# The first modulation in strips of columns turned by VectorE, and two tiles of the second group brought forward into the first stage

## Chip, core and metric

One core of one Trainium2 chip runs the whole program in one launch. The metric is the device time in microseconds (us). The kernel before took 2163.56 us, the median of 3 runs (2163.24 to 2165.64).

## What is computed

Two layers of one mixer block run over 640 tokens: 512 latent tokens (modulated by a vector c) and 128 context tokens (modulated by c_ctx). The width is D = 2048. The part of the reference that the change touches, for each layer:

```
mod  = silu(cond) @ w_mod[l] + b_mod[l]          # 2048 x 6144, for two vectors: c and c_ctx
shift, scale, gate = split(mod, 3)
xn   = rmsnorm(x, norm_w) * (1 + scale) + shift
proj = xn @ w_in[l]                              # 2048 -> 5664 columns
... attention (8 heads), convolution, gated linear attention (GLA) on parts of proj ...
x    = x + gate * (concat(A, B, C) @ w_out[l])
```

## The kernel before, in words

Everything is float32. A product of full width is made of three products in the fast format fp32r: each operand is split in a high part (rounded) and a low part (the rest), and high*high + high*low + low*high is summed in PSUM. "Cast" below is ScalarE's copy that makes the high part of a weight chunk (L1249), "low" is VectorE's subtraction (L1748).

The work of each layer is: front projection, attention with more projection tiles between its steps (L822), GLA with the first half of the output projection as filling (`fill`, L1050), second half of the output projection (`half_tile`, L843). Each engine has its own program, written out by hand, in fixed order; semaphores join them. SyncE (SP) issues nearly all loads, in order, and a wait in its queue holds all loads behind it.

**Front projection.** 8 groups of 4 tiles (512 columns of `w_in` each). A group walks k, the 2048 rows, in 8 chunks of 2 x 128 rows. So there are 64 chunks, numbered 0 to 63; chunk n belongs to group n // 8. A chunk is one load of 512 KB into a ring of 4 slots (`ring`, L369), one cast, one low, and 5 pieces on TensorE (`front_piece`, L771): one for each of the 4 tiles over the 512 latent tokens, one for the 128 context tokens. A piece is 2 rows of k times 3 products, 6 matmuls of 512 columns. Chunk n can be cast when chunk n - 4, the one before it in its slot, is done on TensorE (L1246). A group's sums stand in PSUM `psP` (4 tiles) and `psT` (context). ScalarE takes them out (`take_group`, L1260) and stores them; it does so in its program after cast 8g + 10, and the first piece of the next group's tile m waits for tile m to be taken (L779).

**First modulation (layer 0, shift and scale).** 32 MB of `w_mod` come through four buffers `wmod` of 1 MB, one for each quarter q of k. They make 8 blocks t of 512 columns; t = 2j and 2j + 1 give scale and shift of the 4 rows of x in block j. `mod_quarter(t, q)` (L695) makes 4 float32 matmuls of 512 columns with the two conditioning vectors as weights; each of the 4 has its own strip of 32 PSUM partitions, so a quarter's k are spread over the strips, and the strips must be summed later. ScalarE copies the result to SBUF (`mod_row`, L1204), TensorE sums the strips and turns them with 4 small matmuls against `fold` (`mod_turn`, L705), ScalarE takes that (`mod_take`, L1211), VectorE adds the bias (`mod_sum`, L1755). Two PSUM places are used in turn. Then ScalarE applies scale and shift to x (L1337) and VectorE splits it (L1784, L1786). TensorE's program (L914 to L929) puts pieces of group 0 between the quarters of t = 2 to 7; the pieces of block j run beside the loads of block j + 1.

**Other modulation.** Gate of layer 0 and shift and scale of layer 1 are summed by VectorE in chunks 8 to 63: 16 units of 4 quarters, a quarter being 8 operations (`mod_quarter` of VectorE, L1704). `quarters_at` (L112) says after which chunk's low they run: 8 quarters in 7 chunks. VectorE may start a unit when TensorE has added up the strips of the unit two before it (L1710; `mod_strips`, L849, at the chunks `STRIPS_AT`). Layer 1 uses the same table for its gate. After chunk 63 VectorE forms x again from its parts (L1885), TensorE reads it in `gate_ranks` (L745), and all engines meet in a fence (L396) before attention.

Of the kernel before, what the change touches and what calls it, by code (L numbers as in the profile page):

```python
# [24 lines left out]
P = 128  # L25
# [3 lines left out]
DEPTH = 2  # L29
# [65 lines left out]
PIECES_AFTER, PIECES_LAST = [0, 2, 0, 2, 0, 2, 0, 1], 3  # L95
assert sum(PIECES_AFTER) + PIECES_LAST == BLOCK_C * PIECES and len(PIECES_AFTER) == 8
# [90 lines left out]
NAMES = """gla_lr_in x_part0 x_part1 rows_in x_in consts_in rows_turned vecs_ready head_ready embed_turned x_taken  # L187
# [7 lines left out]
chunk_in0 chunk_in1 chunk_in2 chunk_in3 chunk_cast chunk_split chunk_done latent_done latent_taken  # L195
# [15 lines left out]
def backbone(nc, io):  # L211
    with ExitStack() as ctx:
# [22 lines left out]
        fold = sb("fold", [P, P // 4])  # L235
# [99 lines left out]
        mod_rows = [sq_sum[:, 0:MOD_N], r_b[:, 0:MOD_N]]  # L335
# [33 lines left out]
        def ring(pair, n):  # L369

            at = n % RING
            return pair[at // 2][:, at % 2 * KT // 2:(at % 2 + 1) * KT // 2, :].rearrange("p a b -> p (a b)")\
                .rearrange("p (k n) -> p k n", n=GROUP_N)
        rs_ps = [psT[:, 0:512], psO[:, 512 + 2 * P:512 + 3 * P]]
        mod_ps, mod_back = [psT[:, 512:512 + MOD_N], psO[:, 0:MOD_N]], psO[:, 512:512 + 2 * BLOCK_K]
# [29 lines left out]
        def _(sp):  # L405
# [18 lines left out]
            def front_chunk(l, n):  # L424

                at = n + l * FRONT_CHUNKS
                first, k = FRONT[n // CHUNKS][0], n % CHUNKS * CHUNK_K
                if n < RING:
                    sp.wait_ge(s[f"split{n // 2}"], l * per_layer + SEED)
                else:  # L430
                    sp.wait_ge(s["chunk_split"], at - RING + 1)
                sp.dma_start(ring(raw, n), io["w_in"][l].rearrange("(k p) n -> p k n", p=P)
                             [:, k:k + CHUNK_K, first * P:first * P + GROUP_N]).then_inc(s[f"chunk_in{n % RING}"], 16)

            for t in range(MOD_CHUNKS):
                mod_block(t)
                front_chunk(0, t)

# [13 lines left out]
            for l in range(DEPTH):  # L452
# [51 lines left out]
                sp.wait_ge(s["chunk_split"], (l + 1) * FRONT_CHUNKS - 2)  # L504
                conv_weights(0, 0)
                value_in(0)
                sp.wait_ge(s["chunk_split"], (l + 1) * FRONT_CHUNKS)
# [177 lines left out]
        def _(pe):  # L685
            def spread(out, lhsT, rhs, start=True, stop=True):

                pe.matmul(out[:, 0:512], lhsT, rhs[:, 0:512], start=start, stop=stop)
                return pe.matmul(out[:, 512:TOK], lhsT, rhs[:, 512:TOK], start=start, stop=stop)

# [4 lines left out]
            def mod_quarter(t, q):  # L695

                if q == 0 and t >= 2:
                    pe.wait_ge(s["mod_row"], t - 1)
# [6 lines left out]
            def mod_turn(t):  # L705

                pe.wait_ge(s["mod_row"], t + 1)
                pe.wait_ge(s["mod_taken"], t + SEED)
                for j in range(BLOCK_K):
                    mm = pe.matmul(mod_back[:, 2 * j:2 * j + 2], mod_rows[t % 2][:, j * P:(j + 1) * P], fold[:, 0:2],  # L710
                                   start=True, stop=True)
                mm.then_inc(s["mod_turned"], 1)
# [5 lines left out]
            pe.wait_ge(s["ones_set"], 4)  # L718
            pe.wait_ge(s["x_in"], 16 * TT)
            pe.wait_ge(s["vecs_ready"], DEPTH)  # L720
# [11 lines left out]
            for q in range(4):  # L732
                mod_quarter(1, q)
                if q == 0:
                    pe.wait_ge(s["x_squared"], 2 * TT + 2)
                    mod_turn(0)
            mod_turn(1)
# [33 lines left out]
            def front_piece(l, n, m):  # L771

                g, c = l * len(FRONT) + n // CHUNKS, n % CHUNKS
                whole, rest = ring(high, n), ring(low, n)
                if m == 0:
                    pe.wait_ge(s["chunk_split"], n + l * FRONT_CHUNKS + 1)
# [23 lines left out]

            def block_piece(n):

                front_piece(0, n // PIECES, n % PIECES)
# [45 lines left out]
            def mod_strips(l, u):  # L849

                pe.wait_ge(s["mod_acc"], u + l * UNITS + 1 + SEED)
                if u == 0:
                    pe.wait_ge(s["mod_taken"], l + MOD_CHUNKS + SEED)
                    pe.wait_ge(s["ones_set"], 4 + 3 * (l + 1))
# [9 lines left out]
            def units_turn(l):  # L864

                pe.wait_ge(s["mod_row"], l + MOD_CHUNKS + 1)
# [29 lines left out]
            for l in range(DEPTH):  # L896
# [13 lines left out]
                else:  # L910
# [3 lines left out]
                    for t in range(2, MOD_CHUNKS):  # L914
                        for q in range(4):
                            mod_quarter(t, q)
                            if t % 2 == 1 and q == 0:
                                mod_turn(t - 1)
# [3 lines left out]
                        if t % 2 == 1:  # L922
                            mod_turn(t)
# [3 lines left out]
                    while piece < CHUNKS * PIECES:  # L927
# [153 lines left out]
                for pr in range(PAIRS):  # L1081
# [109 lines left out]
        def _(act):  # L1191
# [12 lines left out]
            def mod_row(t):  # L1204

                act.wait_ge(s["wmod_used3"], t + 1 + SEED)
                if t >= 2:
                    act.wait_ge(s["mod_turned"], t - 1)
                act.activation(mod_rows[t % 2], mod_ps[t % 2], ACT.Copy).then_inc(s["mod_row"], 1)

            def mod_take(t):  # L1211

                act.wait_ge(s["mod_turned"], t + 1)
                act.activation(mod_raw[:, 0, mod_at(t):mod_at(t) + BLOCK_K, :].rearrange("p a b -> p (a b)"), mod_back,
                               ACT.Copy).then_inc(s["mod_taken"], 1)

# [10 lines left out]
            for l in range(DEPTH):  # L1227
                act.wait_ge(s["rows_turned"], l + 2)
                act.activation(vecs[:, l, :], psP[l][:, 0:ROWS], ACT.Copy).then_inc(s["vecs_ready"], 1)
# [11 lines left out]
            def cast_ring(l, n):  # L1241

                at = n + l * FRONT_CHUNKS
                act.wait_ge(s[f"chunk_in{n % RING}"], 16 * (at // RING + 1 + l * SLOT_FILLS[n % RING]))
                if n >= RING:
                    act.wait_ge(s["chunk_done"], at - RING + 1)  # L1246
                elif l > 0:
                    act.wait_ge(s[f"tile_done{n // 2}"], l * per_layer - 1 + n % 2 + SEED)
                act.activation(ring(high, n), ring(raw, n), ACT.Copy).then_inc(s["chunk_cast"], 1)  # L1249

            for l in range(DEPTH):
# [7 lines left out]

                def take_group(g):  # L1260
# [3 lines left out]
                    for m in range(GROUP_T):  # L1264
# [1023 lines left out]
```

## Time and profile before

| what | value |
|---|---|
| median of 3 runs | 2163.56 us |
| profiled execution, its own time | 2162.03 us |
| its span | 2160.1 us |
| TensorE (PE) busy | 2118.3 us, 98% |
| VectorE (DVE) busy | 1403.7 us, 65% |
| ScalarE (ACT) busy | 649.2 us, 30% |
| GpSimd (POOL) busy | 190.6 us, 9% |
| mean DMA rate | 168 GB/s |
| first 54 us / next 54 us of the span | 355 / 387 GB/s |

The profiled execution lasted 1.93 us longer than its span. A busy TensorE isn't TensorE at its peak: the matmuls overlap, and the time of a stretch is read from start to start. A line that is that of a helper stands for many places; tiles and times tell them apart.

### The profile page before, as it was taken

What the parts mean: (1) busy time and instruction counts of PE and PEld (TensorE: products, weight loads), DVE (VectorE), ACT (ScalarE), POOL (GpSimd) and SP (SyncE); (2) the same over time, 40 slices, a digit from 0 to 9 for tenths busy, and PEclk for the clock granted to TensorE, in tenths of its full rate; (3) what the DMA queues carried; (4) which work ended last, traced back from release to release, by engine and by line L of the source; (5) the groups of instructions that cost most, each with busy time, mean ns of one, the idle gap of its engine ahead of it and who ended that gap; (6) DMA issues with size and microseconds to landing.
All of it is one profiled execution on the core that took longest, in us unless ns stands there. A gap on an engine that the chain in (4) does not pass through costs nothing.

```text
span 2160.1 us, 33866 instructions
## 1 busy us (share of the span) xinstructions
PE 2118.3 (98%) x13255; PEld 1886.6 (87%) x13255; DVE 1403.7 (65%) x2739; ACT 649.2 (30%) x1104; POOL 190.6 (9%) x125
## 2 busy tenths in 40 slices
PE   5999999999999999999999999999999999999998
PEld 3578887887999999999998888888899999999998
DVE  5469878999565666765357555455666566676654
ACT  4332221321333334443034122132133333343302
POOL 0000000000000000423321000000000000042331
PEclk9999999999999999999999999999999999999999
DMA  9999687664433324564445646544343233366444
GB/s 355 387 309 307 197 287 244 210 217 153 121 105 89 100 87 130 186 212 129 127 125 173 190 139 193 151 131 132 113 129 104 75 97 105 99 210 195 140 123 151
DMA packets 355216, 363.25 MB, mean 168 GB/s; under 512 B 17606, under 2 KB 262044, under 8 KB 354460
## 3 DMA queue, kind: packets, MB, share of 16 engines
q1 hardware_dynamic: 326416, 318.57, 47.4%
q10 hardware_dynamic: 28684, 43.09, 5.5%
q8 instruction: 78, 1.28, 0.2%
q14 instruction: 38, 0.31, 0.0%
HBM read 302.89 MB, written 58.72 MB: 167 GB/s over the span
## 4 chain that ended last, share of the span: by engine, by line
PE 89%; DVE 4%; DMA 3%; issue 2%; ACT 1%; ACTq 0%; SPq 0%; DVEq 0%
PE psP L787 32%; PE psP L822 20%; PE psP L843 9%; PE psT L797 8%; PE psO L1050 5%; PE psO L1023 3%; PE psP L978 2%; PE psT L1050 2%; DMA wmod<-in_w_mod_dram 2%; PE psT L989 2%; DVE old L2021 1%; PE psT L701 1%; PE psP L725 1%; PE psO L859 1%; DVE second_low L1690 0%
## 5 line engine op out<-in xcount | busy, mean ns | idle before, releaser
L1730 DVE SCALAR_TENSOR_TENSOR macc<-mraw,cond,macc 128x384 f32<-128x384 f32 (+1 forms) x960 | 389.1, 476 | 0.0
L787 PE MATMUL psP<-x_high,high 128*128 128x512 f32 x896 | 356.2, 398 | 0.6 <-DVE x_low L1786 0.6
L787 PE MATMUL psP<-x_high,low 128*128 128x512 f32 x896 | 349.8, 390 | 0.0
L787 PE MATMUL psP<-x_low,high 128*128 128x512 f32 x896 | 349.8, 390 | 0.0
L1249 ACT ACTIVATE high<-raw 128x1024 fp32r<-128x1024 f32 x128 | 135.5, 1059 | 550.3 <-PE psT L797 512.8
L822 PE MATMUL psP<-x_high,high 128*128 128x320 f32 x1024 | 242.6, 318 | 0.0
L822 PE MATMUL psP<-x_high,low 128*128 128x320 f32 x1024 | 233.4, 309 | 0.0
L822 PE MATMUL psP<-x_low,high 128*128 128x320 f32 x1024 | 233.1, 309 | 0.0
L787 PEld LDWEIGHTS psP<-x_high,high 128*128 128x128 f32 x896 | 168.6, 188 | 49.4 <-issue 10.5
L1748 DVE TENSOR_TENSOR low<-raw,high 128x1024 fp32r<-128x1024 f32 x128 | 163.1, 1274 | 73.5 <-ACT high L1249 73.5
L787 PEld LDWEIGHTS psP<-x_high,low 128*128 128x128 f32 x896 | 168.6, 188 | 35.9
L787 PEld LDWEIGHTS psP<-x_low,high 128*128 128x128 f32 x896 | 168.8, 188 | 33.9 <-issue 0.5
L822 PEld LDWEIGHTS psP<-x_high,low 128*128 128x128 f32 x1024 | 171.1, 188 | 0.0
L822 PEld LDWEIGHTS psP<-x_low,high 128*128 128x128 f32 x1024 | 171.0, 188 | 0.0
L822 PEld LDWEIGHTS psP<-x_high,high 128*128 128x128 f32 x1024 | 167.5, 188 | 0.6 <-issue 0.5
L2191 POOL MEMSET cu<- 128x643 f32 x2 | 1.3, 635 | 1588.0 <-DVEq L396 1588.0
L1050 PE MATMUL psO<-x_high,high 128*128 128x320 f32 x704 | 134.8, 313 | 2.1 <-DVE old L2021 2.1
L1720 DVE TENSOR_SCALAR macc<-mraw,cond 128x384 f32<-128x384 f32 (+1 forms) x64 | 19.7, 349 | 158.0 <-PE psO L859 129.7
L843 PE MATMUL psP<-second_high,high 128*128 128x320 f32 x512 | 116.9, 310 | 1.8 <-DVE low L1683 1.8
L843 PE MATMUL psP<-second_low,high 128*128 128x320 f32 x512 | 116.8, 309 | 0.0
L843 PE MATMUL psP<-second_high,low 128*128 128x320 f32 x512 | 116.6, 309 | 0.0
L1050 PEld LDWEIGHTS psO<-x_high,high 128*128 128x128 f32 x704 | 109.4, 188 | 6.1 <-DVE old L2021 3.9
(319 smaller groups left out, 3615.6 us busy)
## 6 DMA issues: line engine op xcount, KB each, us to landing
raw<-in_w_in_dram SPq DMA_DIRECT2D x128, 512.0 KB, 4.9
wmod<-in_w_mod_dram SPq DMA_DIRECT2D x32, 1024.0 KB, 9.9
mraw<-in_w_mod_dram SPq DMA_DIRECT2D x64, 512.0 KB, 4.3
mraw<-in_w_mod_dram SPq DMA_DIRECT2D x32, 1024.0 KB, 7.6
raw<-in_w_in_dram SPq DMA_DIRECT2D x32, 1024.0 KB, 6.2
raw<-in_w_out_dram SPq DMA_DIRECT2D x64, 512.0 KB, 4.5
old<-x_scratch SPq DMA_DIRECT2D x64, 320.0 KB, 3.2
xf<-proj_scratch SPq DMA_DIRECT2D x48, 320.0 KB, 3.6
```

The source lines that it names most:

```text
L701: mm = pe.matmul(mod_ps[t % 2][32 * k:32 * k + 2, :], cond[:, q * KT // 4 + k, :], wmod[q][:, k, :], start=(q == 0), stop=(q == 3), skip_g ...
L787: mm = pe.matmul(latent_ps[m], own, moved, start=(k == 0 and w is whole and x is x_high), stop=(k == KT - 1 and w is rest))
L797: mm = pe.matmul(prompt_ps, x[:, k, DEC:TOK], w[:, kk, :], start=(k == 0 and w is whole and x is x_high), stop=(k == KT - 1 and w is rest))
L822: mm = pe.matmul(psP[0][:, AT + half * HALF:AT + (half + 1) * HALF], w[slot][:, k, :], x[:, k, half * HALF:(half + 1) * HALF], start=(k == ...
L843: mm = pe.matmul(out[:, AT + half * HALF:AT + (half + 1) * HALF], w[slot][:, at + k, :], x[:, k, half * HALF:(half + 1) * HALF], start=(k ...
L978: mm = pe.matmul(score_ps[:, part], q[:, i * P:(i + 1) * P], x[:, part], start=(q is q_high and x is k_high), stop=(q is q_low))
L989: mm = pe.transpose(psT[:, j * P:(j + 1) * P], probs[i % 2][:, j * P:(j + 1) * P], ident[:])
L1023: pe.matmul(psO[:, 0:DEC], v[:, j, :], x[:, j, :], start=(j == 0 and v is vals_high and x is probs_high), stop=(j == KEYS // P - 1 and v i ...
L1050: mm = pe.matmul(out[:, AT + half * HALF:AT + (half + 1) * HALF], w[slot][:, at + k, :], x[:, k, half * HALF:(half + 1) * HALF], start=(k ...
L1249: act.activation(ring(high, n), ring(raw, n), ACT.Copy).then_inc(s["chunk_cast"], 1)
L1730: m = dve.scalar_tensor_tensor(acc[:, v, 0:width], mraw[hf][:, k, 0:width], c, acc[:, v, 0:width], ALU.mult, ALU.add)
L1748: dve.tensor_tensor(ring(low, n), ring(raw, n), ring(high, n).bitcast(F32), ALU.subtract)\
```

## The change

The constants:

```diff
-PIECES_AFTER, PIECES_LAST = [0, 2, 0, 2, 0, 2, 0, 1], 3
+EXTRA_T, EXTRA_PIECES = 2, 4
+PIECES_AFTER, PIECES_LAST = [0, 2, 1, 2, 1, 2, 1, 2], 3
+EXTRA_SLOT = RING - 1
```

**First modulation.** Every k now makes 4 matmuls of 128 columns, one for each strip b; strip b holds the columns 32b to 32b + 31 of each of the 4 rows, and all k are added up in PSUM. One VectorE transpose of 32 x 32 blocks gives the result turned. `mod_row`, `mod_turn`, `mod_take` and `fold` are gone. There is one PSUM place, not two, so quarter (t, 0) waits for the turn of t - 1.

```diff
+                if q == 0 and t > 0:
+                    pe.wait_ge(s["mod_turned"], t)
                 pe.wait_ge(s[f"wmod_in{q}"], t * 16 + 16)
                 for k in range(KT // 4):
-                    mm = pe.matmul(mod_ps[t % 2][32 * k:32 * k + 2, :], cond[:, q * KT // 4 + k, :], wmod[q][:, k, :],
-                                   start=(q == 0), stop=(q == 3), skip_group_check=True)
+                    at = q * KT // 4 + k
+                    parts = wmod[q][:, k, :].rearrange("p (j b c) -> p b j c", b=P // FLIP, c=FLIP)
+                    for b in range(P // FLIP):
+                        mm = pe.matmul(mod_ps[FLIP * b:FLIP * b + 2, :], cond[:, at, :], parts[:, b],
+                                       start=(at == 0), stop=(at == KT - 1), skip_group_check=True)
...
+                    def flip(t):
+                        dve.wait_ge(s["wmod_used3"], t + 1 + SEED)
+                        dve.transpose(mod_turn[t % 2], mod_ps).then_inc(s["mod_turned"], 1)
...
                     scale_block(0)
-                    chunk_low(0)
                     for j in range(BLOCKS):
+                        flip(2 * j)
+                        chunk_low(BLOCK_C * j)
+                        flip(2 * j + 1)
+                        dve.wait_ge(s["mod_turned"], 2 * j + 2)
...
+                        dve.wait_ge(s["chunk_cast"], extra_turn(j) + 1)
+                        dve.tensor_tensor(extra_slot(low), extra_slot(raw), extra_slot(high).bitcast(F32), ALU.subtract)\
+                            .then_inc(s["chunk_split"], 1)
```

**Two tiles of group 1.** Its tiles 0 and 1 walk all of k in the first stage, 4 pieces a block, between the chunks 2j and 2j + 1, into `psO`. Their weights (4 loads of 512 KB) use slot 3 of the ring; group 0 has 3 slots. So a chunk of group 0 frees slot n % 3, and chunk 9 (slot 1) now waits for chunk 7. In group 1 the chunks have 3 pieces in place of 5; they are loaded and cast in full.

```diff
+def slot_user(l, n):
+    if n < RING:
+        return n - EXTRA_SLOT if l == 0 and n >= EXTRA_SLOT else None
+    if l == 0 and n < CHUNKS:
+        return n - EXTRA_SLOT
+    if l == 0 and n < CHUNKS + RING:
+        return [m for m in range(CHUNKS) if chunk_slot(0, m) == n % RING][-1] if n % RING < EXTRA_SLOT else "extra"
+    return n - RING
...
             def cast_ring(l, n):
+                user = slot_user(l, n)
+                if user == "extra":
+                    act.wait_ge(s["extra_done"], BLOCKS)
+                elif user is not None:
+                    act.wait_ge(s["chunk_done"], user + l * FRONT_CHUNKS + 1)
...
                 for n in range(FRONT_CHUNKS):
                     if l > 0 or n >= CHUNKS:
-                        for m in range(PIECES):
+                        for m in range(EXTRA_T if l == 0 and n // CHUNKS == 1 else 0, PIECES):
                             front_piece(l, n, m)
...
+                    if l == 0 and n == CHUNKS + RING:
+                        for e in range(EXTRA_T):
+                            take_latent(1, e, extra_ps[e])
```

In the stretch left out above, VectorE adds the bias and splits x as before (`mod_sum`, four `split_x`, chunk 2j + 1's low between them).

**VectorE's quarters**, in both layers: 4 in the 8 chunks of group 1, then 60 in 48 chunks.

```diff
+    def done(j):
+        return j * 4 // CHUNKS if j <= CHUNKS else 4 + (j - CHUNKS) * 4 * (UNITS - 1) // (MOD_SPAN - CHUNKS)
-    return range(j * 4 * UNITS // MOD_SPAN, (j + 1) * 4 * UNITS // MOD_SPAN) if j >= 0 else range(0)
+    return range(done(j), done(j + 1)) if j >= 0 else range(0)
```

**GLA and output projection**, in both layers (the first wait of the second pair stands ahead of the product `qt`, the second ahead of `kt_`):

```diff
-                        fill(f + 7, 0, 1)
+                        fill(f + 7, 0, 2)
                         turn_back(gp)
-                        fill(f + 7, 1, HALF_K)
+                        fill(f + 7, 2, HALF_K)
...
-                    dve.wait_ge(s["g_factors"], gp * 2 + 2)
+                    dve.wait_ge(s["g_factors"], gp * 2 + 1)
...
+                    dve.wait_ge(s["g_factors"], gp * 2 + 2)
...
-                    low_half(f + 5)
+                        if i == TT - 3:
+                            low_half(f + 5)
...
+                second_weights(0, 1)
                 for j in range(2):
                     sp.wait_ge(s[f"x_part{j}"], 16 * (l + 1) * OUT_PAIRS + SEED)
-                for j in range(2):
-                    old_x(j, 0)
-                with sp.Fori(1, OUT_PAIRS) as i:
-                    for j in range(2):
-                        second_weights(j, i)
-                        sp.wait_ge(s[f"taken{j}"], i + occ + SECOND + SEED)
-                        old_x(j, i)
+                    old_x(j, 0)
+                with sp.Fori(1, OUT_PAIRS - 1) as i:
+                    second_weights(1, i)
+                    sp.wait_ge(s["taken0"], i + occ + SECOND + SEED)
+                    old_x(0, i)
+                    second_weights(0, i + 1)
+                    sp.wait_ge(s["taken1"], i + occ + SECOND + SEED)
+                    old_x(1, i)
...
```

## Rows read from the trace of the kernel before

**Rows 1.** A stretch: length, busy us (instructions) by engine, TensorE's clock, DMA share, GB/s
```profile
49.00:56.00 7.00, 6.43 (x22) 3.50 (x25) 6.90 (x11) 2.40 (x4) 0.00 (x0) 0.57 1.05 387
```
**Rows 2.** Timeline of TensorE, one block: start, length, engine, line, operation [idle before]
```profile
86.33 1.05 PE L710 MATMUL psO<-fold,sq_sum 128*128 128x2 f32 x8
87.32 1.04 PE L701 MATMUL psO<-wmod,cond 128*2 128x512 f32 x8
...
92.61 1.04 PE L701 MATMUL psO<-wmod,cond 128*2 128x512 f32 x8 [0.34 <-DMA wmod<-in_w_mod_dram]
...
95.08 0.95 PE L710 MATMUL psO<-fold,r_b 128*128 128x2 f32 x8
95.88 0.49 PE L787 MATMUL psP<-x_high,high 128*128 128x512 f32 x1
...
110.71 1.05 PE L710 MATMUL psO<-fold,sq_sum 128*128 128x2 f32 x8
```
**Rows 3.** The chain that ended last, in order of time: start, us, what
```profile
131.40 5.44 PE psP L787 x24
138.20 5.44 PE psP L787 x24
...
414.70 5.44 PE psP L787 x24
```
**Rows 4.** Timeline of TensorE after the front projection
```profile
536.37 1.29 PE L745 MATMUL psO<-xf,lr_w 128*32 128x160 f32 x32 [0.26 <-DVE x_last L1885]
```
**Rows 5.** Timeline of the start, all engines
```profile
39.66 3.03 DVE L1793 TENSOR_TENSOR x_hat<-xf,rstd 128x640 f32<-128x640 f32 x4
39.73 4.53 SPq L421 DMA_DIRECT2D wmod<-in_w_mod_dram  x4
...
49.56 1.88 PE L701 MATMUL psT<-wmod,cond 128*2 128x512 f32 x8 [1.59 <-DMA wmod<-in_w_mod_dram]
51.38 0.80 PE L787 MATMUL psP<-x_high,high 128*128 128x512 f32 x1
```
**Rows 6.** Timeline of ScalarE where group 0 ends
```profile
135.06 1.06 ACT L1249 ACTIVATE high<-raw 128x1024 fp32r<-128x1024 f32 x1 [0.26 <-DMA raw<-in_w_in_dram]
136.03 0.58 ACT L1268 ACTIVATE stage<-psP 128x512 f32<-128x512 f32 x1
...
138.23 0.60 ACT L1268 ACTIVATE rstd<-psP 128x512 f32<-128x512 f32 x1 [0.51 <-ACT stage L1268]
```
**Rows 7.** Timeline of VectorE in the front projection
```profile
138.51 1.22 DVE L1748 TENSOR_TENSOR low<-raw,high 128x1024 fp32r<-128x1024 f32 x1
139.65 4.32 DVE L1730 SCALAR_TENSOR_TENSOR macc<-mraw,cond,macc 128x384 f32<-128x384 f32 x8
...
411.88 1.47 DVE L1837 SCALAR_TENSOR_TENSOR xf<-xf 128x1280 f32<-128x1280 f32 x1
...
414.79 8.55 DVE L1730 SCALAR_TENSOR_TENSOR macc<-mraw,cond,macc 128x384 f32<-128x384 f32 x16
...
428.83 0.75 DVE L1720 TENSOR_SCALAR macc<-mraw,cond 128x384 f32<-128x384 f32 x2 [2.95 <-PE psO L859]
...
511.73 1.23 DVE L1748 TENSOR_TENSOR low<-raw,high 128x1024 fp32r<-128x1024 f32 x1 [0.47 <-ACT high L1249]
...
521.34 1.22 DVE L1659 CAST high<-raw 128x2048 fp32r<-128x2048 f32 x1
```
**Rows 8.** Timeline where attention begins
```profile
550.74 0.28 DVE L1897 TENSOR_TENSOR vals_low<-cv,vals_high 128x128 fp32r<-128x128 f32 x1
...
553.55 0.45 PE L978 MATMUL psP<-k_high,q_high 128*128 128x320 f32 x2
```
**Rows 9.** Waits of TensorE over the span: us in total, times, longest
```profile
PE psO L1050 <- DVE old L2021: 2.1, 8, 0.3
PE psP L843 <- DVE low L1683: 1.8, 2, 1.0
PE psT L1070 <- DVE kt_ L2071: 1.5, 2, 1.1
```

More of the change, by code:

```diff
@@ L334, in backbone @@
                 ytok = sb("ytok", [P, TT, D], F32, last)
-        mod_rows = [sq_sum[:, 0:MOD_N], r_b[:, 0:MOD_N]]
+        mod_turn = [sq_sum[:, i * P:(i + 1) * P] for i in range(2)]
         unit_rows = sq_sum[:, 0:MOD_STEP * P // 2]
@@ L799, in front_piece, with extra_piece @@
                 mm.then_inc(s["chunk_done"], 1)
-            def block_piece(n):
-                front_piece(0, n // PIECES, n % PIECES)
+            def extra_piece(j, i):
+                e, pair = i % EXTRA_T, i // EXTRA_T
+                whole, rest = extra_slot(high), extra_slot(low)
+                if i == 0:
+                    pe.wait_ge(s["x_split"], (j + 1) * BLOCK_K + SEED)
+                    pe.wait_ge(s["chunk_split"], extra_turn(j) + 1)
+                cols = slice(e * P, (e + 1) * P)
+                for kk in range(2 * pair, 2 * pair + 2):
+                    k = j * BLOCK_K + kk
+                    for w, x in ((whole, x_high), (whole, x_low), (rest, x_high)):
+                        mm = pe.matmul(extra_ps[e], w[:, kk, cols], x[:, k, 0:DEC],
+                                       start=(k == 0 and w is whole and x is x_high), stop=(k == KT - 1 and w is rest))
+                if i == EXTRA_PIECES - 1:
+                    mm.then_inc(s["extra_done"], 1)
+            def block_piece(n):
+                j, i = n // BLOCK_PIECES, n % BLOCK_PIECES
+                if i < PIECES:
+                    front_piece(0, BLOCK_C * j, i)
+                elif i < PIECES + EXTRA_PIECES:
+                    extra_piece(j, i - PIECES)
+                else:
+                    front_piece(0, BLOCK_C * j + 1, i - PIECES - EXTRA_PIECES)
             def turn_prompt(g):
@@ L926, in _ @@
                                 piece += 1
-                    while piece < CHUNKS * PIECES:
+                    while piece < BLOCKS * BLOCK_PIECES:
                         block_piece(piece)
@@ L1258, in cast_chunk, with take_latent @@
                     cast_ring(l, n)
+                def take_latent(g, m, src):
+                    first, gate = FRONT[g]
+                    n = l * len(FRONT) + g
+                    tile = n * GROUP_T + m
+                    act.wait_ge(s[f"stored{m % 2}"], (n * GROUP_T // 2 + l * HEADS) * 16 + SEED)
+                    if tile // EXTRA_T == GROUP_T // EXTRA_T:
+                        act.wait_ge(s["extra_done"], BLOCKS)
+                    else:
+                        act.wait_ge(s["latent_done"], tile + 1 - (EXTRA_T if tile > GROUP_T else 0))
+                    act.activation(leaving[m], src, ACT.Silu if gate else ACT.Copy).then_inc(s["latent_taken"], 1)
+                    act.wait_ge(s["latent_taken"], tile + 1)
+                    dst = v_dram[m] if g == BY_TOKEN else proj_dram[first + m][:, 0:DEC]
+                    act.dma_start(dst, leaving[m]).then_inc(s[f"stored{m % 2}"], 16)
                 def take_group(g):
@@ L1263, in take_group @@
                     n = l * len(FRONT) + g
-                    for m in range(GROUP_T):
-                        tile = n * GROUP_T + m
-                        act.wait_ge(s[f"stored{m % 2}"], (n * GROUP_T // 2 + l * HEADS) * 16 + SEED)
-                        act.wait_ge(s["latent_done"], tile + 1)
-                        act.activation(leaving[m], latent_ps[m], ACT.Silu if gate else ACT.Copy)\
-                            .then_inc(s["latent_taken"], 1)
-                        act.wait_ge(s["latent_taken"], tile + 1)
-                        dst = v_dram[m] if g == BY_TOKEN else proj_dram[first + m][:, 0:DEC]
-                        act.dma_start(dst, leaving[m]).then_inc(s[f"stored{m % 2}"], 16)
+                    for m in range(EXTRA_T if l == 0 and g == 1 else 0, GROUP_T):
+                        take_latent(g, m, latent_ps[m])
                     act.wait_ge(s["chunk_done"], (n + 1) * CHUNKS)
@@ L1597, in _ @@
             dve.memset(ones[:], 1.0).then_inc(s["ones_set"], 1)
-            for part in mod_ps:
-                dve.memset(part, 0.0).then_inc(s["ones_set"], 1)
+            dve.memset(mod_ps, 0.0).then_inc(s["ones_set"], 1)
             dve.wait_ge(s["consts_in"], 16 * 5)
-            dve.tensor_reduce(fold[:], ident[:].rearrange("p (a b) -> p b a", a=4), AX.X, ALU.add).then_inc(s["ones_set"], 1)
             def set_pick():
```

148 lines of the change are left out of this document (76 added, 72 removed).

## The prediction

> **What bounds the kernel now.** The page first: TensorE is busy 98% of the span, at full clock in all 40 slices but for one place, so a change gains only what it takes off TensorE's own queue or off its waits. I then read the chain of waits: it is TensorE nearly throughout, at an even pace. A chunk's 30 matmuls of 512 columns take 138.20 - 131.40 = 6.80 us [rows 3], so one piece (6 matmuls) costs 1.36. The first stage is the exception. There the DMA engines are full (share 1.05, 387 GB/s [rows 1]), and TensorE is nearly full too: from one turn to the same turn a block later is 110.71 - 86.33 = 24.38 us [rows 2], with about 0.4 us of wait for data in it (0.34 in the row, a little more by the starts). Two limits are balanced there; removing TensorE work alone would only turn it into waiting for the 9 MB of a block. Last the waits of TensorE: outside the first 50 us they are short, the three that the late edits address being 2.1, 1.8 and 1.5 us in all [rows 9].
>
> **Turns removed, tiles moved in.** The moved tiles are no saving by themselves: 16 pieces x 1.36 = 21.8 us go from group 1 to group 0. They matter because they fill the room that the turns leave. In a block the two `mod_turn` cost 87.32 - 86.33 = 0.99 and 95.88 - 95.08 = 0.80 us [rows 2]. A new block costs TensorE 24.38 - 1.79 - 0.4 + 4 x 1.36 = 27.6, and there are two more places where it goes from pieces to a quarter and back, for which I take 0.3 each, an estimate (the matmul after such a change shows 0.49 us against a pitch of 0.227 [rows 2, 3]): 28.2. The loads of a block grow from 9 to 9.5 MB, 24.38 x 9.5 / 9 = 25.7 us, so they stay below 28.2, and the waits for data go. Gain per block 24.38 + 5.44 - 28.2 = 1.6, for three blocks **-4.8 us**. Bounds: -6.6 if a change of kind costs nothing, -2 if it costs 0.8.
>
> **The quarters in strips.** A quarter has 16 matmuls of 128 columns (32 records) in place of 4 of 512 (8 records): the same columns. The nearest row is `gate_ranks`, also four strips of short float32 matmuls: 32 records of 160 columns in 1.29 us [rows 4], by 128/160 1.03 us, as long as the 1.04 of an old quarter [rows 2]. I take **0**. Upper bound: 1.29 in full, 0.25 x 22 quarters = +5.5; lower bound 0, since no column is saved.
> The Trainium skill ("TensorE: Matmul & The Clock Gate", section "Wait — 56ns, not 53.3ns?") speaks against the change here: start to start never drops below about 25 ns, and with hardware decode off the sequencer spends about 62 ns for each matmul. By the 62 ns a quarter would be 32 x 62 = 1.98 us, and the sum would be some 22 us worse. The row, 1.29 us / 32 = 40 ns for longer matmuls, disagrees with 62 and leaves the 25 open.
>
> **VectorE's turn in place of ScalarE's copies.** A transpose of 128 columns is not in the trace; ScalarE's and TensorE's part that it replaces was off the path but for the turns. Between 0.2 and 1 us each; in blocks 1 to 3 it stands behind five pieces or two (6.8 or 2.7 us), which hide it. VectorE's block (2 turns, sums, 4 splits, 3 lows, 3.03 us of scaling) is about 15 us of 28, so it is not late. Exception: t = 1. One PSUM place means that quarter (1, 0) waits for the turn of t = 0, which stands behind the scaling of block 0, 39.66 + 3.03 = 42.7 [rows 5]. TensorE ran it at once before. So the buffers come free near 43.9 in place of 39.73 [rows 5]. The DMA engines still have chunk 1 and now 0.5 MB for the moved tiles in queue, so they idle only about 1.5 us; quarter (2, 1) comes at about 51.0 in place of 49.56 [rows 5], and the first piece moves from 51.38 likewise: **+1.4** (0 to +4; the upper end if the clock, 0.57 in this stretch [rows 1], falls during the longer lull and quarter t = 1 runs at half pace).
>
> **The hand-over from group 0 to group 1.** Chunk 9 now uses the slot of chunk 7, so its cast waits for TensorE's last piece of group 0. In ScalarE's program cast 9, cast 10, then the four takes follow one another. TensorE's next piece is tile 2 of chunk 8, which waits for three takes. Cast to next operation is 136.03 - 135.06 = 0.97, take to take (138.23 - 136.03) / 2 = 1.10 [rows 6]. So: 0.2 + 2 x 0.97 + 2 x 1.10 + 0.60 = 4.9, with the signal 5.0 us in which TensorE has nothing to do. Before, the takes lay in the time of the last pieces: chunk 8 began at 138.20 [rows 3] with the first take done at 136.6. **+5.0**. Upper bound +8.4, if the clock falls after this lull for as long as at 48 to 55 us (0.57 over 7 us is 3.4 us lost if busy); I put **+1.0** for it. Lower bound +3.9 (a shorter queue of takes).
>
> **Quarters of VectorE.** A low costs 139.65 - 138.51 = 1.14, a quarter 8.47 / 2 = 4.24, the first of a unit 3.84 [rows 7]. Group 1's chunks now last 3 x 1.36 = 4.1 us, and half a quarter each fits (3.3). After it, 4 chunks hold 5 quarters: 4 x 1.14 + 5 x 4.24 - 0.5 = 25.3, against 4 x about 7.1 = 28.4 us of TensorE; with the key normalisation some 4 us more in places. So VectorE isn't the bound but lives with little room, and it ends later. Unit 11 now begins at chunk 48, after the strips of chunk 46, about 415.4 (chunk 47 starts at 414.70 [rows 3]). Against the kernel before at 414.79 it has still to do one quarter (3.84), one low (1.14), the 414.79 - 411.88 = 2.91 us of chunk 49, and in chunks 49 to 63 one quarter more (19 for 18, and less 0.4 for an earlier unit start: 3.8); it saves the three waits of 2.95, 4.18 and 0.47 = 7.6 us [rows 7] (the first and last of the three). End of the quarters: 521.34 + 0.6 + 3.84 + 1.14 + 2.91 + 3.8 - 7.6 = 526.0 to 526.5, some 5 us later. The forming of x (16 operations) and the fence before attention follow it. TensorE waited 0.26 us for it already [rows 4]. Where attention begins, VectorE's last preparation ended at 551.02 and TensorE's scores began at 553.55 [rows 8]: 2.4 us of slack. **+2.6** (0 to +6). Layer 1's quarters are a third as wide; nothing there.
>
> **Late edits.** The weights of tile 1 no longer stand in SP's queue behind the stores: the 1.8 us [rows 9] go, what is late next is the add before it, hidden by a half tile. The factor product starts one exponential (1.25 us) earlier: the 1.5 us for `kt_` go. `low_half` in an idle place of VectorE: of the 2.1 us some 1.2 go. The turn back stands one k (0.9 us) later; its chain has about 1 us of slack: 0. Together **-4.5** (-5.4 to -1.5).
>
> **Sum.** -4.8 + 0 + 1.4 + 5.0 + 1.0 + 2.6 - 4.5 = +0.7 us. On the profiled execution's own time 2162.03 (2160.1 span and 1.9 around it) that is 2162.7; the runs' median is 1.5 higher, so 2163.56 + 0.7, **2164.3 us**: no change that can be told. A measurement of this kernel can tell about 0.2%, 4.3 us.
>
> **Rivals.**
> (a) Faster: the hand-over costs little, because TensorE would otherwise have waited there or the takes run sooner, and VectorE's lag is absorbed. Then -4.8 + 1.4 - 4.5 = -7.9, **2155.7**. For it: the two main costs are read from program order, not from a row. Against: each link of the hand-over is a wait that stands in the diff. 0.33.
> (b) Slower, one mechanism: VectorE becomes the bound of groups 2 to 7. From 48 chunks x 7.1 = 341 us it needs 48 x 1.14 + 60 x 4.24 - 6 + 13 (keys) = 316, plus its waits for strips and for `mraw`. If these waits exceed 25 us (40 were spent before), each further us is TensorE's. With 8 more, 2164.3 + 8 = **2172**. It decides from a low that ends after its chunk could start; I reckon the smallest margin at 2 us. 0.19.
> (c) The short matmuls are bound by their issue: +5.5, **2170**. 0.06. By the skill's 62 ns it would be 2186, which I put at 0.01 within this.
> (d) The first stage stays bound by loads (3 slots, queue of SP), so the new pieces displace nothing: +5, **2169**. 0.05.
> The forecast has 0.37, with its own range 2160 to 2168.
>
> **How the numbers follow.** Faster (below 2159.3): nearly all of (a) and a little of the forecast, 0.35. Slower (above 2167.9): most of (b), (c), (d) and the forecast's edge, 0.28. Same: 0.37. The range 2154 to 2173 takes (a) and (b) in and leaves out 0.2.
>
> **What would show it.** No L710 rows, and blocks of about 28 us with no wait for `wmod` after 55 us; quarters of 0.9 to 1.1 us. An idle stretch of about 5 us of TensorE before the first piece of chunk 8, ended by ScalarE's take L1268 (its line may shift), with the clock after it. VectorE's last quarter some 5 us late against TensorE's chunk 63, and a wait of TensorE for x in `gate_ranks`. No TensorE wait of over 0.5 us in GLA. The forecast is wrong if that stretch is absent, or if chunks 16 to 63 show waits for a low.

## The result, and the profile after

The changed kernel takes **2167.04 us** (median of 20 runs, 2165.74 to 2170.15), the kernel before 2163.47 (20 runs, 2162.30 to 2165.64). The ratio is 1.0018 (95% interval 1.0012 to 1.0024): slower by 3.9 us, small but clear of the noise. The forecast was 2164.3 in a range of 2154 to 2173. The profiled execution took 2167.36 us, its span 2165.6, 5.5 longer than that of before.

The waits of TensorE over the span, as in [rows 9] (us in total, times, longest):

```profile
...
PE psP L839 <- ACT rstd L1332: 4.9, 1, 4.9
PE psO L755 <- DMA head_rows<-in_final_norm_w_dram: 4.3, 1, 4.3
PE psT L766 <- DVE sq_sum L1871: 4.3, 1, 4.3
PE psT L766 <- DMA wmod<-in_w_mod_dram: 3.8, 2, 2.6
PE psO L1123 <- DVE old L2108: 2.0, 4, 0.7
...
```

Two of them are new: 4.9 us for the third take of group 0 (`rstd` is its buffer), and 4.3 us for the turn of t = 0 (`sq_sum` holds `mod_turn`). The waits for `kt_` and for the low of the second half are gone.

The timeline of TensorE, the start and one block, to be held against [rows 2] and [rows 5]:

```profile
37.82 0.39 PE L787 MATMUL psO<-r_a,ones 128*128 128x128 f32 x2
42.48 5.82 PE L766 MATMUL psT<-wmod,cond 128*2 128x128 f32 x128 [4.27 <-DVE sq_sum L1871]
49.47 1.06 PE L766 MATMUL psT<-wmod,cond 128*2 128x128 f32 x32 [1.17 <-DMA wmod<-in_w_mod_dram]
53.15 1.36 PE L766 MATMUL psT<-wmod,cond 128*2 128x128 f32 x32 [2.62 <-DMA wmod<-in_w_mod_dram]
54.44 0.80 PE L839 MATMUL psP<-x_high,high 128*128 128x512 f32 x1
...
103.62 0.50 PE L839 MATMUL psP<-x_high,high 128*128 128x512 f32 x1
...
110.64 1.93 PE L766 MATMUL psT<-wmod,cond 128*2 128x128 f32 x64
112.50 0.50 PE L839 MATMUL psP<-x_high,high 128*128 128x512 f32 x1
...
132.03 0.50 PE L839 MATMUL psP<-x_high,high 128*128 128x512 f32 x1
```

A block now takes 132.03 - 103.62 = 28.41 us, with no wait for data. Two quarters take 112.50 - 110.64 = 1.86 us with the change to the next piece in it, 29 ns for each of the 64 records on average. Where quarters stand back to back they start 0.87 us apart, and 0.86 us in the kernel before: the strips cost nothing that counts. The records don't come evenly: four start within 0.02 us of each other, one for each strip, and the next four 0.109 us later. The first piece comes at 54.44 in place of 51.38.

Stretches of the start and of the hand-over, columns as in [rows 1]:

```profile
40.00:42.00 2.00, 0.00 (x0) 0.00 (x0) 2.00 (x3) 0.00 (x0) 0.00 (x0) 0.52 1.06 399
42.00:44.00 2.00, 1.52 (x32) 1.06 (x36) 1.53 (x3) 0.35 (x1) 0.00 (x0) 0.50 1.01 354
44.00:46.00 2.00, 2.00 (x44) 1.40 (x40) 0.00 (x0) 0.71 (x1) 0.00 (x0) 0.50 0.36 66
46.00:48.00 2.00, 2.00 (x64) 1.55 (x56) 0.00 (x0) 0.00 (x0) 0.00 (x0) 0.77 0.94 333
...
158.00:163.00 5.00, 0.16 (x1) 0.00 (x0) 3.66 (x7) 3.68 (x5) 0.00 (x0) 1.00 0.25 29
163.00:166.00 3.00, 2.90 (x7) 2.35 (x8) 2.54 (x4) 1.43 (x3) 0.00 (x0) 0.50 0.98 371
```

While TensorE waits for the turn, its clock falls to 0.50; the first two quarters of t = 1 then take 1.7 us each (they start at 42.48 and 44.14, the third at 45.84) in place of 0.87, the buffers come free late, and the loads sink to 66 GB/s. After the 5 us at 158 the clock is 0.50 again.

ScalarE's timeline at the hand-over, to be held against [rows 6]:

```profile
158.26 2.00 ACT L1311 ACTIVATE high<-raw 128x1024 fp32r<-128x1024 f32 x2 [11.16 <-PE psT L849]
160.17 0.58 ACT L1332 ACTIVATE stage<-psP 128x512 f32<-128x512 f32 x1
...
161.26 0.60 ACT L1332 ACTIVATE stage<-psP 128x512 f32<-128x512 f32 x1 [0.52 <-ACT stage L1332]
...
162.36 0.60 ACT L1332 ACTIVATE rstd<-psP 128x512 f32<-128x512 f32 x1 [0.51 <-ACT stage L1332]
```

It shows each link of the forecast: two casts in 1.91 us, started when TensorE ends group 0, then three takes 1.10 apart. TensorE begins again at 163.10, as the third ends.

VectorE: the turn that TensorE waited for, and the end of its quarters (compare [rows 7]):

```profile
39.16 3.03 DVE L1866 TENSOR_TENSOR x_hat<-xf,rstd 128x640 f32<-128x640 f32 x4
42.11 0.31 DVE L1871 STREAM_TRANSPOSE sq_sum<-psT 128x128 f32<-128x128 f32 x1
...
521.87 8.56 DVE L1803 SCALAR_TENSOR_TENSOR macc<-mraw,cond,macc 128x384 f32<-128x384 f32 x16
530.34 1.22 DVE L1732 CAST high<-raw 128x2048 fp32r<-128x2048 f32 x1
```

Where the difference of the two profiled executions arises, by the start of the same matmul on TensorE:

| point | before | after | difference |
|---|---|---|---|
| first piece of group 0 | 51.38 | 54.43 | +3.05 |
| context piece of chunk 63 | 533.89 | 538.75 | +4.86 |
| first filling in GLA, layer 0 | 852.13 | 858.10 | +5.97 |
| layer 0's second half, its 145th matmul | 1016.65 | 1020.81 | +4.16 |
| context piece of chunk 0, layer 1 | 1124.02 | 1130.40 | +6.38 |
| end of layer 1's second half | 2139.82 | 2143.71 | +3.89 |
| end of the span | 2160.1 | 2165.6 | +5.5 |

### The profile page after: what moved, and what is told of

Read it like the earlier page. It is cut to its first block, busy times and chain, and to the rows that moved or that the text cites. A ratio compares the mean times of both kernels' runs of the same rounds, so it can differ in the third digit from the quotient of the medians.

```text
span 2165.6 us, 35256 instructions
## 1 busy us (share of the span) xinstructions
PE 2117.5 (98%) x13959; PEld 1903.3 (88%) x13959; DVE 1412.2 (65%) x2749; ACT 647.7 (30%) x1092; POOL 194.2 (9%) x125
## 4 chain that ended last, share of the span: by engine, by line
PE 88%; DVE 8%; issue 2%; DMA 1%; ACT 1%; ACTq 0%; SPq 0%; DVEq 0%
PE psP L839 27%; PE psP L896 20%; PE psP L917 10%; PE psT L849 7%; PE psO L1123 6%; DVE macc L1803 3%; PE psT L1123 3%; PE psO L1096 3%; PE psP L1051 3%; PE psT L1062 2%; PE psT L766 1%; PE psO L864 1%; DVE low L1821 1%; DVE xf L1972 1%; PE psP L781 0%
## 5 line engine op out<-in xcount | busy, mean ns | idle before, releaser
L839 PE MATMUL psP<-x_high,high 128*128 128x512 f32 x864 | 343.7, 398 | 5.0 <-ACT rstd L1332 4.9
L839 PE MATMUL psP<-x_high,low 128*128 128x512 f32 x864 | 337.5, 391 | 0.0
L839 PE MATMUL psP<-x_low,high 128*128 128x512 f32 x864 | 337.5, 391 | 0.0
L839 PEld LDWEIGHTS psP<-x_high,high 128*128 128x128 f32 x864 | 162.9, 189 | 46.7 <-issue 12.2
L839 PEld LDWEIGHTS psP<-x_high,low 128*128 128x128 f32 x864 | 162.8, 188 | 34.8
L839 PEld LDWEIGHTS psP<-x_low,high 128*128 128x128 f32 x864 | 163.0, 189 | 32.9 <-issue 0.5
L896 PEld LDWEIGHTS psP<-x_high,low 128*128 128x128 f32 x1024 | 171.1, 188 | 0.0
L896 PEld LDWEIGHTS psP<-x_low,high 128*128 128x128 f32 x1024 | 171.0, 188 | 0.0
L896 PEld LDWEIGHTS psP<-x_high,high 128*128 128x128 f32 x1024 | 167.6, 188 | 0.6 <-issue 0.5
```

The source lines that it names most:

```text
L839: mm = pe.matmul(latent_ps[m], own, moved, start=(k == 0 and w is whole and x is x_high), stop=(k == KT - 1 and w is rest))
L896: mm = pe.matmul(psP[0][:, AT + half * HALF:AT + (half + 1) * HALF], w[slot][:, k, :], x[:, k, half * HALF:(half + 1) * HALF], start=(k == ...
```

## The experiments

All ratios are to the kernel before, timed on the same chip; experiments 1 to 4, 5 to 8 and 9 to 11 ran on three different chips, so that times of different groups are compared by their ratios.

**1. The late edits alone**, put into the kernel before (the fourth block of the diff above and nothing else).

> The kernel before with the late edits alone (weights of tile 1 ahead of the stores, the split wait of the factor product, low_half in the loop, the turn back one k later). Theory: they give what the two profiles show between GLA and the end of the second half, 0.6 + 1.2 us in layer 0 and 1.4 + 1.1 us in layer 1, so 4.3 us: 2159.2, ratio 0.998. Rival: the gain in the changed kernel belongs to another phase of the work, and alone they give under 1 us: ratio 0.9995 or more.

2159.35 us, ratio 0.9981 (0.9972 to 0.9990): 4.1 us gained, as the theory has it. No wait for `kt_` or for a low of the second half is left. So the rest of the change costs 0.37%, 8.0 us.

**2. The takes ahead of the cast of chunk 9**, in the changed kernel:

```diff
                 for n in range(RING + (KT - CAST_FROM) // 2, FRONT_CHUNKS + RING):
+                    if l == 0 and n == CHUNKS + 1:
+                        for m in range(GROUP_T):
+                            take_latent(0, m, latent_ps[m])
```

(and `take_group(0)` leaves them out)

> The changed kernel, but the four takes of group 0's latent tiles stand ahead of the cast of chunk 9 in ScalarE's program. Theory: the idle stretch of TensorE at the hand-over (5.1 us) and the half clock after it (1.6 us) are this order of ScalarE alone, both go: 2167.0 - 6.7 = 2160.3. Rival: TensorE then waits for the cast and the low of chunk 9 or 10 or their loads, or VectorE's lag grows by what TensorE gains and comes back at the start of attention: only 2 to 3 us, 2164.5.

2159.43 us, ratio 0.9983 (0.9974 to 0.9992): 7.6 us less than the changed kernel. ScalarE now takes each tile while TensorE works on the next, and casts chunk 9 when group 0 ends:

```profile
153.40 0.60 ACT L1332 ACTIVATE stage<-psP 128x512 f32<-128x512 f32 x1 [5.72 <-PE psP L839]
...
156.12 0.60 ACT L1332 ACTIVATE rstd<-psP 128x512 f32<-128x512 f32 x1 [0.76 <-DMA proj_scratch<-stage]
...
158.84 2.01 ACT L1311 ACTIVATE high<-raw 128x1024 fp32r<-128x1024 f32 x2 [0.76 <-PE psT L849]
```

TensorE has no idle stretch there and no half clock after it. The gain was above the 6.7 of the two; in the profiled executions a stretch at the lower clock where layer 1 begins was shorter as well (3.4 against 6.8 us).

**3. The turn of t = 0 ahead of the scaling of block 0**, in the changed kernel:

```diff
+                    flip(0)
                     scale_block(0)
                     for j in range(BLOCKS):
-                        flip(2 * j)
+                        if j > 0:
+                            flip(2 * j)
```

> The changed kernel, but VectorE turns t = 0 ahead of the scaling of block 0. Theory: TensorE's wait of 4.3 us before quarter (1, 0) shrinks to about 1.2 us, the buffers come free 3 us earlier, the clock keeps its full level there, and the first piece starts at 51.4 in place of 54.4: 2167.0 - 3.0 = 2164.0. Rival: the first piece is bound by the 32 MB that come anyway, the loads of t = 2 are not sooner: under 0.7 us, 2166.5.

2165.38 us, ratio 1.0007 (0.9998 to 1.0016): 2.4 us less by the ratios, whose intervals just touch, near the theory's 3.0. The wait fell to 1.3 us and the clock stayed full while t = 1 ran, but the first piece started at 53.68, not 51.4: TensorE now waits 5.2 us for the first load of t = 2, and the clock falls in that wait instead, for 10.4 us from 47.1 us on.

**4. Both moves together.**

> The changed kernel with both moves (takes ahead of cast 9, turn of t = 0 ahead of the scaling). Theory: the two add up, 2167.0 - 9.7 = 2157.3, ratio to the kernel before 0.9971. Rival: VectorE, whose quarters end later than before, becomes the bound once TensorE is 10 us earlier, and the wait for x before attention takes 3 us or more back: 2160.5.

2157.59 us, ratio 0.9971 (0.9960 to 0.9982), 10.2 us less than the changed kernel by the ratios: they add up. VectorE did not take anything back beyond the wait of 0.5 us for `x_last`.

**5. Strips and turn without the moved tiles**: `EXTRA_PIECES` = 0, group 0 with four slots, the old pieces and the old table of quarters; the late edits stay.

> The first modulation in strips with VectorE's turn, and the late edits, but no moved tiles: group 0 has its 4 slots, the old pieces after each quarter and the old table of VectorE's quarters. It is to be held against the late edits alone (2159.35). Theory: the loads of 9 MB bound the block of 24.4 us, so the 1.8 us of turns per block become waits for wmod: -0.5 a block; the ramp costs some 2 us as before: 2160. Rival: the loads had followed TensorE, not led it, and a block shrinks by the whole 1.8 us: 2156.

2160.46 us, ratio 0.9989 (0.9980 to 0.9998): 1.7 us above experiment 1 by the ratios, with intervals that overlap. The theory had the sum right and its parts not: a block takes, context piece to context piece, 99.33 - 76.27 = 23.1 and then 23.9 us, against 24.35 in experiment 1, but the ramp (the time up to the first piece) is worse: the first piece starts at 55.06 against 52.75. Waits of TensorE up to 130 us, experiment 1, then this one:

```profile
PE psT L707 <- DMA wmod<-in_w_mod_dram: 2.9, 2, 1.6
PE psO L707 <- DMA wmod<-in_w_mod_dram: 1.7, 3, 1.1
PE psO L716 <- ACT r_b L1215: 0.7, 1, 0.7
```

```profile
PE psT L756 <- DMA wmod<-in_w_mod_dram: 6.1, 6, 2.8
PE psT L756 <- DVE sq_sum L1852: 4.3, 1, 4.3
```

The turns had cost 1.8 us a block; about half of it came back as shorter blocks, the rest as waits for `wmod`.

**6. VectorE's old table of quarters** in the changed kernel:

```diff
-    return range(done(j), done(j + 1)) if j >= 0 else range(0)
+    return range(j * 4 * UNITS // MOD_SPAN, (j + 1) * 4 * UNITS // MOD_SPAN) if j >= 0 else range(0)
```

> The changed kernel with the table of VectorE's quarters of before (8 quarters in 7 chunks from chunk 8 on). Theory: group 1's chunks last 4.1 us, 8 lows and 9 quarters need 8 x 1.14 + 9 x 4.24 = 47 us against 33 of TensorE and 10 of lead, so TensorE waits some 4 to 6 us in chunks 11 to 15, and the lag before attention (1.0) goes: 2171, and waits of TensorE for low in group 1. Rival: the lead of VectorE at the hand-over covers it: 2166.

2169.08 us, ratio 1.0027 (1.0017 to 1.0038): 2 us more than the changed kernel, in the right direction and half of what was expected, but the two intervals overlap. The trace shows the mechanism: TensorE waited for a low in chunks 15 and 16, and no longer for `x_last` in layer 0. Part of the cost in the trace is the clock: at the hand-over it was low for 6.9 us (from 161.6 us on) in place of 3.4. Its waits from 158 to 200 us:

```profile
PE psP L839 <- ACT rstd L1332: 4.9, 1, 4.9
PE psP L839 <- DVE low L1821: 1.7, 1, 1.7
```

**7. The first load of the moved tiles behind the loads of t = 2**, on top of both moves:

```diff
                 mod_block(t)
+                if t == 2:
+                    extra_tiles(0)
                 front_chunk(0, t)
-                if t % 2 == 1:
+                if t % 2 == 1 and t > 1:
                     extra_tiles(t // 2)
```

> The kernel with both moves, and the moved tiles' first load put behind the four wmod loads of t = 2 in SP's queue. Theory: the first piece of group 0 waits for the second quarter of t = 2, which stands behind these 0.5 MB; it comes 1.4 us earlier, and so does everything behind: 2157.6 - 1.4 = 2156.2. Rival: x_low of block 0 comes last there (0.6 us was waited for it): 0.3 us, 2157.3.

2157.37 us, ratio 0.9975 (0.9965 to 0.9984): no difference to experiment 4. The first piece did start 1.36 us earlier (51.63 against 52.99). But the clock differs; stretches of experiment 4, then of this one:

```profile
50.00:52.00 2.00, 1.42 (x28) 0.69 (x24) 1.97 (x4) 1.77 (x3) 0.00 (x0) 0.50 1.05 407
52.00:54.00 2.00, 2.00 (x36) 1.45 (x25) 1.97 (x3) 0.00 (x0) 0.00 (x0) 0.89 1.05 398
```

```profile
50.00:52.00 2.00, 2.00 (x33) 1.25 (x26) 1.97 (x4) 0.80 (x2) 0.00 (x0) 0.50 1.06 398
52.00:54.00 2.00, 2.00 (x6) 1.54 (x6) 1.13 (x2) 0.00 (x0) 0.00 (x0) 0.50 1.04 396
54.00:56.00 2.00, 2.00 (x7) 1.60 (x6) 0.00 (x0) 0.00 (x0) 0.00 (x0) 0.60 1.08 399
```

The first pieces came earlier into a stretch at half clock, which lasted 6.9 us here and 3.4 there; the context piece of chunk 15 starts at 187.78 against 187.30. So in this pair of profiles the clock took the 1.4 us back. Over all runs the mean granted clocks of the two kernels (0.9965 here, 0.9961 there) don't show such a loss, so whether this holds for the medians stays open.

**8. VectorE's quarters end two chunks earlier**, on top of experiment 7 (`MOD_SPAN - CHUNKS - 2` in `done`, and at most 64).

> As load_late, and the last 60 quarters of VectorE end two chunks earlier (46 chunks in place of 48). Theory: VectorE's forming of x and its preparation of attention are late by 1.0 us because its last quarters end late; with 4 us or more of lead the waits for x_last (0.5) and for the first scores (0.4) go in layer 0: 1 us below load_late. Rival: the closer quarters make TensorE wait for a low near chunk 32, where the margin was 1.4 us: 1 to 2 us above load_late.

2156.62 us, ratio 0.9973 (0.9962 to 0.9984): not to be told from experiment 7. In the trace layer 0's wait for `x_last` is gone and one for a low of 0.2 us is new; either theory's effect was too small to be timed.

**9 and 10. The stall alone**, in the kernel of experiment 1. `stall_one` has the first edit, `stall_three` both:

```diff
-                    act.wait_ge(s["chunk_done"], at - RING + 1)
+                    act.wait_ge(s["chunk_done"], at - RING + 1 + (2 if at == CHUNKS + 1 else 0))
...
-                        pe.wait_ge(s["latent_taken"], (g - 1) * GROUP_T + m + 1)
+                        pe.wait_ge(s["latent_taken"], (g - 1) * GROUP_T + m + 1 + (2 if n == CHUNKS and m == 0 and l == 0 else 0))
```

> The late edits alone (2159.35), and in group 0's hand-over the cast of chunk 9 waits for chunk 7 as in the changed kernel; TensorE's first piece of chunk 8 waits for one take. Theory, the same links as in the forecast: 0.2 + 2 casts x 0.97 + one take 0.6 = 2.8 us idle, the later takes (1.10 apart) come within the pieces of 1.36; with no or little fall of the clock 2162.2 to 2163.0. Rival: the wait for chunk 7 costs nothing as long as the weights of chunk 8 are split, since casts and takes are short: 2159.5.

> As stall_one, and TensorE's first piece of chunk 8 waits for three takes, as in the changed kernel. Theory: 2.8 + 2 x 1.10 = 5.0 us idle, and with the fall of the clock after it 1.6 or more: 2159.35 + 6.6 = 2166.0, the whole of what the move of the takes gave back in the changed kernel. Rival: the clock falls only because the first stage of the changed kernel already held low stretches; here it holds: 2164.4.

2163.13 us (ratio 0.9997, 0.9988 to 1.0006) and 2166.36 (1.0011, 1.0002 to 1.0020), against 2159.35: 3.8 and 7.0 us by the medians, 3.5 and 6.5 us by the ratios. The wait that TensorE gained in each:

```profile
PE psP L793 <- ACT stage L1274: 2.7, 1, 2.7
```

```profile
PE psP L793 <- ACT rstd L1274: 4.9, 1, 4.9
```

2.7 and 4.9 us of waiting, and in both the clock falls to its lower level for 3.4 us after it. So the stall costs about 7 us in the old surroundings too, and the rival about the clock falls.

**11. Experiment 5 with the turn of t = 0 first.**

> turn_only (strips turned by VectorE, late edits, no moved tiles) with the turn of t = 0 ahead of the scaling. It is to be held against the kernel with both moves (2157.6), which has the moved tiles as well. Theory: the ramp comes 2 us earlier than in turn_only, the blocks stay bound by their loads: 2158.4, so that the moved tiles are worth about 1 us. Rival: the moved tiles bring nothing or cost, since TensorE's room was already used up: 2157.0 or less.

**2156.41 us**, ratio 0.9964 (0.9950 to 0.9977), 5.4 us less than experiment 5 by the ratios, and the lowest median of all (5 runs; experiments 4, 7 and 8 can't be told from it). Against the kernel with both moves, which has the moved tiles too (0.9971), there is no clear difference; the number is the rival's. In the profiled executions the moved tiles do bring the context piece of chunk 15 forward, 187.30 against 189.77; at the end of the span, 2155.8 against 2156.1, little of it is left. Of the 2.5 us experiment 4 loses 0.9 between chunk 63 and GLA, where VectorE is late, and it has two stretches of 3.4 us at the lower clock (from 1107.1 and from 2137.9 us on) that experiment 11 has not. So this one pair of profiles doesn't say that the moved tiles are worth nothing. Against experiment 1 the strips and the turn, well placed, are worth 3.7 us by the ratios, whose intervals overlap a little.

## Why the prediction was right, and where it was not

The time and the reason were near: a gain in the first stage and in the late edits, given back by a stall of ScalarE's order. That the total came so near is in part luck: the forecast lacked two terms (+2.2 and +1.6) and had the ramp too low, while VectorE's term was 1.5 too high. By its steps, in the two profiled executions, whose own times differ by more (5.3 us) than the medians (3.6):

| step | forecast | measured |
|---|---|---|
| first stage | -4.8 | -4.8 |
| quarters in strips | 0 | 0 |
| ramp | +1.4 | +3.05 |
| hand-over, idle | +5.0 | +5.1 |
| clock after it | +1.0 | +1.6 |
| VectorE's lag before attention | +2.6 | +1.1 |
| late edits | -4.5 | -4.2 |
| lower clock at the start of layer 1 | none | +2.2 |
| end of the program | none | +1.6 |
| sum | +0.7 | +5.5 |

The last column adds up to 5.65; the rest is rounding and 0.1 us that layer 1's front projection took less.

- **First stage.** From the first piece to the end of group 0 it was 138.03 - 51.38 = 86.65 us (the first matmul of chunk 8 starts at 138.03; the 138.20 of [rows 3] is where the chain changes over). Now it is 158.00 - 54.43 = 103.57 (its last matmul starts at 157.77, one pitch of 0.23 earlier) with 16 pieces (21.76) more: -4.8. It isn't three equal blocks: -2.1 up to the context piece of chunk 1, then -1.4 and -1.3 for a block, and nothing in the last stretch. The block took 28.41 against the forecast 28.2, so a change between quarters and pieces cost (28.41 - 27.63) / 2 = 0.4 us where the forecast had 0.3 (27.63 is its sum without these changes).
- **Strips.** A quarter with the change to a piece behind it took 0.97 from start to start in the kernel before, now 0.93 to 0.99; back to back it is 0.86 and 0.87. The Trainium skill ("TensorE: Matmul & The Clock Gate", section "Wait — 56ns, not 53.3ns?") tells of about 62 ns for each matmul with hardware decode off and a floor near 25 ns; the 62 ns do not hold here, whether one counts records (0.87 us / 32 = 27 ns) or the program's matmuls (0.87 us / 16 = 55 ns). The mean of 27 ns lies above the floor, but single starts do not: records of different strips start 7 ns apart. By the 62 ns and the forecast's own 22 quarters the loss would have been 0.94 x 22 = 20.7 us, not 22.
- **Ramp.** This step failed in its size. The forecast had the DMA engines idle for 1.5 us; they fell to 66 GB/s at 44 to 46 us and to 305 at 48 to 50. The missing term is the clock: it fell while TensorE waited for the turn, the first two quarters of t = 1 ran at half pace (the upper end of the forecast's range), and quarter (2, 1) came at 53.15, not 51.0. Experiments 3 and 4, whose code is the same up to there, take that wait away and have the first piece at 53.68 and 52.99, so 0.8 to 1.4 of the 3.05 us are shown to come from the place of the turn. What the rest is stays open. Experiment 7 takes 1.36 us by moving the additional load back, but experiment 11, which has no such load, has its first piece at 53.73, no earlier than experiment 4. The start of the turn of t = 0 alone differs by up to 0.9 us between kernels that are the same up to it (42.11 here, 42.97 in experiment 6).
- **Hand-over.** Right in each link: from the start of group 0's last matmul (157.77) to that of the next (163.10) it is 5.33 us, less the pitch of 0.23 that is 5.1 us of idle. Experiments 9 and 10 rebuild it elsewhere and get 2.7 and 4.9. The term for the clock was a little low: 12 matmuls of chunk 8 took 4.35 us in place of 2.72, +1.6 for +1.0. (Its upper bound took 0.57 over 7 us as 3.4 us lost; that is 7 x 0.43 = 3.0.) Experiment 2 takes all of it away.
- **VectorE.** Its quarters end at 530.3, 9.0 us later, and TensorE is 4.9 us later at chunk 63, so its lag grew by 4.1 us; the forecast had 4.7 to 5.2. Another 1.1 us of it is made up before attention: VectorE's last preparation ends at 558.96 against 551.02, 3.1 us late against TensorE. The slack was about what the forecast took: from there to the first scores it was 2.53 us by [rows 8] (the forecast wrote 2.4) and is 559.32 - 558.96 = 0.36 now. So it was the lag that the forecast had too large, not the slack that it had too small, and only 1.1 us came (0.5 of it the wait for `x_last`). It is not the bound of groups 2 to 7: the smallest margin of a low was 1.4 us at chunk 32 (forecast 2), and TensorE waited for none. Rival (b) did not happen. Experiment 6, whose old table brings waits of up to 1.7 us, shows how near VectorE is to being the bound at the end of group 1 and the start of group 2, not in the groups after.
- **Late edits.** 5.97 - 4.16 = 1.8 us in layer 0, 6.26 (where its gate begins) - 3.89 = 2.4 in layer 1; experiment 1 has 4.1 by itself. The split was off: the wait for `old` stayed at 2.0 us, while the second half gained 1.2 and 1.1 us.
- **Not in the forecast.** In the changed kernel's profile the clock is 0.50 from 1116 to 1122 us, at layer 1's start, where it was 1.00 before:

```profile
1114.00:1116.00 2.00, 1.81 (x14) 1.54 (x12) 0.11 (x1) 1.60 (x2) 0.00 (x0) 0.82 0.00 0
1116.00:1118.00 2.00, 2.00 (x9) 2.00 (x10) 0.74 (x5) 0.21 (x1) 0.00 (x0) 0.50 0.00 0
1118.00:1120.00 2.00, 2.00 (x12) 2.00 (x11) 0.00 (x0) 0.00 (x0) 0.00 (x0) 0.50 0.00 0
```

The same work takes longer there (30 transposes, L970, 4.35 us for the 3.51 of before): matmul for matmul, TensorE's delay against the kernel before grows from 4.2 to 7.2 us, and 0.8 of it comes back right behind. The instructions there are the same in both kernels. Over all runs the mean granted clock was 0.9948 in the changed kernel (20 runs) and 0.9966 in the kernel before (29 runs beside experiments 1 to 4); 0.0018 x 2165 / 0.5 = 7.8 us more at the lower level, worth at most 3.9 us. Part of that is the ramp and the hand-over. Why the clock falls at the layer's start in some kernels and executions (in the changed kernel and in experiments 2, 3, 4 and 8; not in the kernel before nor in 1, 5, 6, 7, 9, 10 and 11) stays open.

The end of the program was 1.6 us longer, and the profiles speak against chance. From the start of the last matmul of layer 1's second half to the end of the span it is 20.3 us in the profiles of the kernel before and of experiments 1, 9 and 10, which have the old first modulation, and 21.5 to 22.1 us in the changed kernel and in experiments 2 to 8 and 11, which have the new one. TensorE isn't the cause: in the changed kernel it does this stretch in the same time. The stores of the output are issued no later, but the last of them lands 21.45 us after that start in place of 19.89. Why they take longer stays open.

Rival (a) is ruled out by the row of 4.9 us, (c) by the quarters of 0.87 us, (d) by blocks with no wait for `wmod`.

## What to carry to other kernels

When work is moved from one phase into another, go through each queue at the seam: here a slot's new predecessor made one cast wait, and everything behind it in ScalarE's program, the takes that TensorE needed, came late; moving four instructions was worth 7.6 us, more than any other part of the change (the late edits 4.1, strips and turn 3.7). Before moving work, try the change without it: strips and turn alone, with the first turn ahead of the scaling, could not be told from the version with the moved tiles. A stall is to be priced with the clock after it, 1 to 2 us more here than the stall itself.

## What the runs showed of the hardware that was not expected

- Float32 matmuls of 128 columns and 2 weight columns, laid in four strips, start four at a time, 7 ns apart; the next four start after 109 ns at full clock and after 213 ns at the lower one (t = 1 of the changed kernel). The time follows the clock, so a fixed time for each matmul is not what limits them.
- A wait of 2.7 us of TensorE after long full work was followed by 3.4 us at half clock, like one of 4.9 us (experiments 9 and 10): there the price of the clock did not grow with the wait. In experiment 6 the same wait of 4.9 us went with 6.9 us at half clock. The waits of 0.5 us and less before attention brought none, nor did the one of 1.7 us in experiment 6.
- VectorE's transpose of 128 x 128 float32 from PSUM in blocks of 32 took 0.31 us.
- Loads ran at 399 to 410 GB/s over stretches of 2 us in several kernels, with TensorE idle (399 at 40 to 42 us of the changed kernel) as well as busy throughout (409 at 56 to 58 us), against 387 in [rows 1].
